# Attention heads with their 12 score units taken in pairs, the split of w_out_2 moved into head 14, and the last half merge moved from GpSimd to VectorE

## The reference, cut to what matters here

```python
def chunk_causal_attention(q, k, v):          # 16 heads, q and k 96 wide, v 64 wide, CHUNK = 64
    scale = QK_HEAD ** -0.5
    for blk in range(S // Q_BLOCK):
        s = jnp.einsum('bqhd,bkhd->bhqk', qb, k[:, :k_end]).astype(jnp.float32) * scale
        mask = k_chunk[None, :] <= q_chunk[:, None]
        p = jax.nn.softmax(jnp.where(mask, s, -jnp.inf), axis=-1).astype(v.dtype)
        outs.append(jnp.einsum('bhqk,bkhd->bqhd', p, v[:, :k_end]))
...
    merged = gates[:, :, 0] * ya.astype(jnp.float32) + gates[:, :, 1] * yb.astype(jnp.float32)
    h = h + merged.astype(h.dtype) @ w_out[l]
```

## Time and profile before

| what | us |
|---|---|
| median of 3 runs (lowest, highest) | 2829.2 (2828.47, 2833.79) |
| the profiled execution's own time | 2830.83 |
| its span, from the first to the last instruction | 2829.0 |
| mean granted TensorE clock in it | 0.970 |
| PE busy, share of the span | 2657.8, 94% |
| DVE busy | 1596.7, 56% |
| ACT busy | 1200.7, 42% |
| POOL busy | 338.1, 12% |

### The profile page before, as it was taken

How to read it: one execution, slowest core, us unless ns; L and a number is a source line. 1 busy time by engine, 2 the same in 40 slices (tenths; PEclk the granted TensorE clock), 3 DMA queues, 4 the chain that set the end, 5 groups by cost and what they waited for, 6 DMA issues and landing times. The chain is left out here.

```text
span 2829.0 us, 32119 instructions
## 1 busy us (share of the span) xinstructions
PE 2657.8 (94%) x12144; PEld 2094.4 (74%) x12144; DVE 1596.7 (56%) x2120; ACT 1200.7 (42%) x1743; POOL 338.1 (12%) x289
## 2 busy tenths in 40 slices
PE   6999999999999999999999989899999879599993
PEld 5888888888878787777777779897666658477772
DVE  5688888888641323443343333686666543666664
ACT  4234444344340213545235323564555521366661
POOL 0010111101100000000000000133122210342213
PEclk9999999999999999999999999999999989699997
DMA  5333323333245212021121131234322031999997
GB/s 188 112 123 108 108 75 108 108 108 101 75 146 196 78 49 82 30 75 43 55 74 42 49 134 34 88 120 164 113 60 56 13 92 68 364 356 347 355 353 275
DMA packets 209160, 362.65 MB, mean 128 GB/s; under 512 B 51911, under 2 KB 159816, under 8 KB 195320
## 3 DMA queue, kind: packets, MB, share of 16 engines
q1 hardware_dynamic: 193432, 322.94, 33.0%
q0 software_dynamic: 14720, 34.64, 3.2%
q10 hardware_dynamic: 864, 3.15, 0.3%
HBM read 310.72 MB, written 116.93 MB: 151 GB/s over the span
## 5 line engine op out<-in xcount | busy, mean ns | idle before, releaser
L398 PE MATMUL PS<-UHI,WHI 128*128 128x512 f32 x1008 | 415.8, 413 | 4.1 <-DVE ULO L127 4.1
L398 PE MATMUL PS<-ULO,WHI 128*128 128x512 f32 x1008 | 400.2, 397 | 0.0
L398 PE MATMUL PS<-UHI,WLO 128*128 128x512 f32 x1008 | 400.2, 397 | 0.0
L127 DVE TENSOR_TENSOR WLO<-arena,WHI 128x1024 fp32r<-128x1024 f32 x94 | 115.3, 1227 | 215.7 <-ACT WHI L123 215.6
L398 PEld LDWEIGHTS PS<-UHI,WHI 128*128 128x128 f32 x1008 | 190.6, 189 | 52.3 <-issue 5.5
L398 PEld LDWEIGHTS PS<-ULO,WHI 128*128 128x128 f32 x1008 | 190.6, 189 | 47.6 <-issue 5.5
L398 PEld LDWEIGHTS PS<-UHI,WLO 128*128 128x128 f32 x1008 | 190.2, 189 | 46.3
L1500 PE MATMUL PS<-U2HI,WHI 128*128 128x512 f32 x480 | 193.0, 402 | 2.7 <-DVE WLO L127 2.7
L1500 PE MATMUL PS<-U2HI,WLO 128*128 128x512 f32 x480 | 189.4, 395 | 0.0
L1500 PE MATMUL PS<-U2LO,WHI 128*128 128x512 f32 x480 | 189.4, 395 | 0.0
L834 DVE SCALAR_TENSOR_TENSOR RC<-arena,cols,RC 128x1024 f32<-128x1024 f32 x120 | 157.2, 1310 | 10.3 <-issue 0.9
(11 more groups left out here) (465 smaller groups left out, 6019.4 us busy)
## 6 DMA issues: line engine op xcount, KB each, us to landing
arena<-in_w_in SPq DMA_DIRECT2D x88, 512.0 KB, 3.9
xd_dram<-in_x SPq DMA_DIRECT2D x32, 768.0 KB, 6.9
y_dram<-in_x SPq DMA_DIRECT2D x32, 768.0 KB, 6.8
arena<-in_w_gate SPq DMA_DIRECT2D x13, 1024.0 KB
arena<-in_w_up SPq DMA_DIRECT2D x13, 1024.0 KB
arena<-in_w_down SPq DMA_DIRECT2D x13, 1024.0 KB, 13.7
qk_dram<-RA SPq DMA_DIRECT2D x32, 384.0 KB, 2.3
arena<-qk_dram SPq DMA_DIRECT2D x32, 384.0 KB, 4.4
```

The source lines that it names most:

```text
L127: return eng.tensor_tensor(dst, src, hi.bitcast(F32), ALU.subtract)
L398: last = pe.matmul(o[:, h * HALF:(h + 1) * HALF], x[:, k, :], y[:, k, h * HALF:(h + 1) * HALF], start=(k == r == 0), stop=(k == ND - 1 and ...
```

## The change

- PE takes the units of a head in pairs: scores 2b and 2b + 1, the trials that `TRIALS` puts at this b (four at b = 0, two at b = 1, two at b = 2), `turn_tops` (b = 3), `turn_head` (b = 3, 4), then values 2b and 2b + 1.
- ACT takes `features_hi` behind the exponentials 7 and 9 instead of 8 and 9. It does all eight blocks of `merge_weights_hi` in head 14, one behind each exponential from k = 4 on, and none in head 15.
- DVE does all eight `merge_weights_lo` in head 14 and none in head 15. After the last reciprocal it merges half 1 of pair 7 itself, with three operations and a wait for POOL's merge of half 0; POOL no longer does that half.

```diff
+        TRIALS = ((0, 1, 2, 3), (4, 5), (6, 7), (), (), ())
...
                 for h in range(NHEADS):
-                    scores(h, 0)
-                    scores(h, 1)
-                    for k in range(NUNIT):
-                        if k + 2 < NUNIT:
-                            scores(h, k + 2)
+                    for b in range(NUNIT // 2):
+                        scores(h, 2 * b)
+                        scores(h, 2 * b + 1)
                         if h + 1 < NHEADS:
-                            if k < 4:
-                                trial(h + 1, 2 * k)
-                                trial(h + 1, 2 * k + 1)
-                            if k == 6:
+                            for i in TRIALS[b]:
+                                trial(h + 1, i)
+                            if b == 3:
                                 turn_tops(h + 1)
-                        if h + 2 < NHEADS and 7 <= k < 9:
-                            turn_head(h + 2, k - 7)
-                        values(h, k)
+                        if h + 2 < NHEADS and 3 <= b < 5:
+                            turn_head(h + 2, b - 3)
+                        values(h, 2 * b)
+                        values(h, 2 * b + 1)
...
-                        if h == NHEADS - 2 and k >= 8:
-                            merge_weights_hi(k - 8)
-                        if h == NHEADS - 1 and k < 8 and k % 2:
-                            merge_weights_hi(4 + k // 2)
+                        if h == NHEADS - 2 and k >= 4:
+                            merge_weights_hi(k - 4)
                         if k == 7 and h + 1 < NHEADS:
                             tops_hi(h + 1)
-                        if 8 <= k < 10 and h + 2 < NHEADS:
-                            features_hi(h + 2, k - 8)
+                        if k in (7, 9) and h + 2 < NHEADS:
+                            features_hi(h + 2, (k - 7) // 2)
...
-                    for half in range(2):
+                    for half in range(2 if t + 1 < NPAIRS else 1):
...
-                    else:
-                        for k in range(4):
-                            merge_weights_lo(4 * (h + 2 - NHEADS) + k)
+                    elif h + 1 < NHEADS:
+                        for k in range(ND):
+                            merge_weights_lo(k)
                 reciprocals(NPAIRS - 1, 1)
+                dve.wait_ge(s_merged, 2 * NPAIRS - 1)
+                y = YB[(NPAIRS - 1) % 2][:, HALF:]
+                dve.drain()
+                dve.tensor_tensor(y, y, SUMREC[1], ALU.mult)
+                dve.drain()
+                dve.tensor_tensor(y, y, SIG1[(NPAIRS - 1) % 2][:, HALF:], ALU.mult)
+                dve.drain()
+                dve.tensor_tensor(RA[:, NPAIRS - 1, HALF:], RA[:, NPAIRS - 1, HALF:], y, ALU.add)
```

## The result

The changed kernel takes 2836.15 us (median of 17 runs, 2832.42 to 2840.37), the kernel before 2829.29 us (17 runs, 2825.26 to 2833.79) measured beside it. The ratio is 1.0024, 95% interval 1.0017 to 1.0031: 6.9 us slower. The forecast was 2825.7 us and a gain. The measured time lies inside the range, but only because the range was drawn to take in the rival in which POOL is shut out (2835.2), and that rival is what happened.

The account below looks back on a forecast made before the run. PE was taken as the bound, with four waits of 1.44 us a middle head and further waits at the end. Pairs +3.2, head 14 +3.2, head 15 -5.5, tail -6.0: -5.1, so 2830.83 becomes 2825.7 us, range 2817 to 2837.

Parts of the forecast that it names:

- the rival in which POOL is shut out: Pair 6, half 1, end of head 14: POOL waits for DVE's eight splits; +9.5 us, 2835.2 us in all, chance 0.25.
- Head 15: Last head: POOL's operations go between DVE's splits, PE waits only 2.2 us; 24.15 falls to 18.7 us, -5.5.
- its small terms: Head 15: values 0, 4, 6, 7, 8 and 10 wait for exponentials, 2.3 us together.
- values 7: Head 15: a wait of 0.8 us for an exponential; heads 0 to 13: 0.02 us to spare, no wait.
- the large wait: Head 15: PE waits 2.2 us for POOL's merge through ACT, taken as too short for the clock to fall.
- Pairs: Heads 0 to 13: old waits of 1.44 us go, new ones of 1.67 come; +0.23 a head, +3.2 us.
- Trials 2 and 3: Heads 0 to 13: these trials wait for the maxima of trials 0 and 1, 1.27 us lost a head.
- values 10: Heads 0 to 13: only scores 11 cover the exponential of unit 10, about 0.4 us lost a head.
- The bound of +0.5 a head: Heads 0 to 13: upper limit of the pair order's cost, if values 0 and 6 also wait; 7 us lost.
- Head 14: ACT's eight splits there lengthen the head from 18.42 to 21.6 us, +3.2.
- The tail: From PE's last values to the last addition: DVE merges the last half, 12.8 falls to 6.8 us, -6.0.

Follow-up runs that it names:

- e4_wait: The changed kernel, with DVE waiting for POOL's merge of pair 6, half 1 before its eight splits; 2828.01 us, 0.9994 of the kernel before.
- e5_drain: The changed kernel, with a drain of DVE behind each of its eight splits; 2829.50 us, 0.9998 of the kernel before.
- e1_pairs: The kernel before, with only PE's pair order and the new place of `features_hi`; 2835.19 us, ratio 1.0017.
- e2_splits: The kernel before, with only all eight splits of w_out_2 put in head 14; 2833.31 us, ratio 1.0004.
- e9_pairs_spread: e6_spread with PE's units in twos; 2826.58 us, 0.9984 of the kernel before.
- e6_spread: The kernel before, with the last half merge on DVE and the eight splits spread over heads 13 to 15, away from POOL's merges; 2818.17 us, ratio 0.9951.
- e3_tail: The kernel before, with only half 1 of pair 7 merged by DVE; 2830.41 us, ratio 0.9996.
- e11_lag: The changed kernel, with two drains of POOL ahead of its merge of pair 6, half 1; 2837.21 us, 1.0023 of the kernel before.
- e12_late7: e6_spread with trial 7 one unit later, behind scores 6 instead of scores 5; 2810.87 us, 0.9927 of the kernel before.

## Why the prediction was wrong

- **Head 15, the step that failed.** "If POOL's operations go between them, as in pair 7": they did not. Forecast -5.5, measured +3.6, 9.1 of the 11.6 us by which the sum was off. e4_wait and e5_drain show the cause: with POOL first or let in by gaps, head 15 takes 18.1 and 20.8. I had both readings in the trace of before, the shut-out of 5.47 in pair 6 and the turns of 2.03 in pair 7, and chose the second for a merge in pair 6, half 1. The right row was the one of the same merge behind the same reciprocal, and I had named it as a rival at half the forecast's chance. That row stretched to eight splits, 5.47 + 4 x 1.13 = 9.99, gives the 10.00 measured. The rival's total of 2835.2 came as near as it did (2836.15) partly by luck: it held the same price of the pairs, 2.5 us too low.
- The Trainium skill, page "SBUF — State Buffer", section "SBUF: two separate sides", has the pair of ports held for one whole instruction by the one that starts first. Rows of e5_drain agree, with POOL served behind one split (2.06 us). The 10.00 us of the changed kernel do not, if the rule means that the one that waits is next: there all eight splits went through while POOL waited. Read so, the rule has POOL in behind one split, which is what I had forecast; the measurement decides against it for this row.
- **Head 15, its small terms.** Its small waits were put at 2.3; in e4_wait, where nothing else disturbs it, they come to 3.6 by the ends of its matmuls (values 7 alone 0.98, values 0, 2, 8 and 10 about 0.5 each, values 4 and 6 about 0.3 each). Values 2 stood in my sum only with the large wait, and I had left out the time that the first matmul behind each wait takes longer. So even POOL in turns gave no 18.7: e5_drain has 20.8, with 1.64 of still time in front of values 2 (2.2 forecast) and a granted clock of 0.83 from 2262 to 2272, where I had taken such a wait as too short for the clock to go down:

```profile
2262.00:2272.00 10.00, 8.36 (x29) 5.39 (x27) 6.68 (x5) 4.16 (x11) 0.70 (x1) 0.83 0.00 0
```

- **Pairs, right mechanism, wrong size.** Trials 2 and 3: 1.27 forecast, 1.28 measured. Too small were values 7 (0.2 on average against nothing) and values 10 (0.51 against 0.4). By the ends, all waits of a middle head sum to 1.97 us after and 1.58 before, where I had 1.67 and 1.44. A head costs +0.41 instead of +0.23; heads 0 to 13 cost +5.7 instead of +3.2, 2.5 of the 11.6 us by which the sum was off. The bound of +0.5 a head held.
- **Head 14, right in sum, wrong in cause.** +3.2 forecast, +3.6 measured, but I had put all of it on the eight splits. e1_pairs has +2.7 by the order with four splits, and e2_splits +1.2 by the eight with the old order. Together they make 3.9, near the 3.6. The order's part is itself partly lost cover for ACT's splits: with only two splits in head 14 (e9_pairs_spread against e6_spread) it is 1.7.
- **The tail** came as forecast, -5.9 from the last values to the last addition, and -6.4 to PE's restart.
- Without the shut-out the forecast would still have been too good: e5_drain, the run nearest to its case, is 0.5 below before by the trace where I had -5.1, and its ratio is 0.9998 (0.9989, 1.0007).

Open: why POOL and DVE take turns in pair 7, half 0 of before without a gap between the splits (the next starts 0.08 before the end of the one ahead, against 0.07 in pair 6) while in pair 6 they don't. It is no chance of one execution: the trace of e3_tail has both again (2.03 and 5.46 us), that of e1_pairs the turns in pair 7 (2.04). So a gap was enough to let POOL in wherever one was seen or made, but it is not shown that only a gap does. e11_lag speaks against the moment of arrival, from 0.21 to 0.36 us; data and addresses differ between the two places, and I tried neither.

## What to carry to other kernels

When one engine's merge is on the path, ask what row of two-input operations the other runs beside it, and take the same pair of instructions in the same place as the price, not the friendlier one. A row of VectorE without gaps can hold GpSimd out for as long as the row is; with the same order of PE, putting it elsewhere was best here (total 340.3), a wait of VectorE for GpSimd next (341.7), a drain between third (344.7), against 351.6 for the bare row. And taking the steps of a pipeline in twos removes cover as well as waits: here one trial moved by one unit gave 7 us (e12_late7 against e6_spread), and the units in twos cost 8 (e9_pairs_spread against e6_spread).

## What the runs showed of the hardware that was not expected

- A drain behind each operation of VectorE, which sounds like a cost, made the changed kernel faster by 6.9 us (e5_drain, by the trace): it gave GpSimd its turn after 2.06 us instead of 10.00. While they take turns, each VectorE split that shares takes 2.1 to 2.3 us against some 1.2.
- One gap of 0.10 us, between the first two of four splits, was enough for that (e1_pairs: 2.08 us instead of 5.47), and the turns then went on without a further gap.
- The same kind of operation, two inputs of 128 x 512, takes GpSimd 1.26 us and VectorE 0.69 where nothing runs beside it.
